# Stick-breaking attention in pairs of steps: turns and scores in 64-row tiles

## The chip, the cores and the metric

The kernel runs on one core of one Trainium2 chip. The metric is the device time of one execution in microseconds. The engines are named as the profile names them: PE (TensorE; PEld is its loading of weights), DVE (VectorE), ACT (ScalarE), POOL (GpSimd) and SP (SyncE, which here only issues DMAs).

## What is computed

One layer with a stick-breaking attention mixer over 2048 tokens of width 1024, with 16 heads of 64, and a final RMSNorm. All is float32.

```python
def stick_breaking_attention(q, k, v):
    """q,k,v: (B,S,H,Dh). A[t,s] = beta[t,s] * prod_{s<j<t} (1-beta[t,j]), s<t only."""
    ...
        z = jnp.einsum('bthd,bshd->bhts', q[:, t0:kend], k[:, :kend]).astype(jnp.float32) * scale
        mask = s_idx < t_idx
        log_beta = jax.nn.log_sigmoid(z)
        log_rem = jnp.where(mask, jax.nn.log_sigmoid(-z), 0.0)
        after = lax.cumsum(log_rem, axis=3, reverse=True) - log_rem
        w = jnp.where(mask, jnp.exp(log_beta + after), 0.0)
        outs.append(jnp.einsum('bhts,bshd->bthd', w.astype(v.dtype), v[:, :kend]))

def mixer_stick_breaking(h, w_in, w_out):
    proj = jnp.einsum('bsd,de->bse', h, w_in)
    q, k, v, g = jnp.split(proj, 4, axis=-1)
    o = stick_breaking_attention(q.reshape(hs), k.reshape(hs), v.reshape(hs)).reshape(B, S, SB_WIDTH)
    return jnp.einsum('bse,ed->bsd', o * jax.nn.silu(g), w_out)
```

The result is `rmsnorm(x + mixer(rmsnorm(x)))`.

## The kernel before

Every matrix product keeps float32 precision by splitting each operand into an upper part of reduced precision (`..._hi`) and the remainder (`..._lo`) and adding products of parts. The tokens are reversed on the host, so that the sum over later positions becomes a scan forward.

The program has four stretches. Up to about 184 us PE makes the values of all heads (line 713). Then it makes keys, queries and gates, in 96 groups of 24 products of 512 columns (`project`, line 764). From about 211 us the attention runs, with the rest of the projection spread between its steps (`filled(n)`: 3.344 products per step). From about 1466 us the gated output is multiplied with the output weights (`put_out`, line 851) and normalized.

The attention is a list of 640 steps (`STEPS`): for each of 16 heads, for query chunks c of 512 tokens, for key chunks j from c on, for four blocks r of 128 queries. Ten (c, j) units of four steps make a head; in the four units with j = c ("on the diagonal") the score widths of the four steps are 512, 384, 256 and 128 columns, and the widths of their turned pieces too; elsewhere all are 512. A step m passes through six operations:

- `scores` (PE, lines 782 and 784): two 128-row products into one of two banks `z_ps`. `k_parts` holds a head's keys in 64 rows of upper and 64 rows of lower parts, `q_parts` the queries in the same way, and `q_swapped` with the parts exchanged; so the two products sum all four products of parts.
- `stick` (ACT, L1003): the sigmoid, from `z_ps` into `u`.
- `scan` (DVE, L1236): the running product along the keys, in place.
- `turn` (PE, L794): transposes, 128 x 128 each, one for each of the four query blocks of the unit (fewer on the diagonal), into one of three banks `turn_ps`. It needs the scans of all blocks of the unit.
- `hi` (ACT, L1009) and `lo` (DVE, L1241): the upper and the lower part of the turned piece, out of the same bank.
- `weigh` (PE, L810 and L812): two products with the differences of the values (`dv_head`) into `o_ps`, which collects a chunk; `empty` (ACT, L1015) takes it out into one of two tiles `o_stage`.

The order is written by hand. Each engine has a loop over n, in which it does step n + 9 of the scores and sigmoids (`LEAD_SCORES`), n + 6 of the scans (`LEAD_SCAN`), n + 2 of the turns and upper parts (`LEAD_TURN`), and step n of the lower parts and the weighing, with the projection between. On PE a step is: scores, turn, project, weigh; where a score or weighing product has only 128 columns, a turn is put between the two. On DVE it is `made_low` (the lower part of a projection group, L1222 or L1220), scan, `lo`, then other parts such as `weight_lo` (L1212). SP loads keys (lines 528 and 529) and queries (539 and 540) a unit or more ahead; a load waits until the steps that used the place have their scores. At the beginning of the attention, at line 859, eight small transposes of 16 rows turn the first values; they are the only instructions on PE that don't use all 128 rows.

## Time and profile before

| | us |
|---|---|
| median of 3 runs | 1651.32 |
| lowest, highest | 1651.22, 1652.89 |
| the profiled execution | 1651.07 |
| its span, first to last instruction | 1649.3 |
| PE busy | 1638.1 (99%) |
| DVE busy | 1348.6 (82%) |
| ACT busy | 904.7 (55%) |

A row of PE has a start and a length, and the length contains the way of the last column through the array, so products in a row overlap in the records: what a product costs is the distance of its start to the next one's. The same holds on DVE and ACT to a lesser degree. "Idle before" is the time in which an engine had nothing running, and what released it.

### The profile page before, as it was taken

To read this page: it belongs to the slowest core of one execution; us is meant where nothing else is said; L and a number is where in the kernel's file an instruction comes from. 1 tells how busy PE (TensorE), PEld (TensorE's weight loads), DVE (VectorE), ACT (ScalarE), POOL (GpSimd) and SP (SyncE) were. 2 spreads that over 40 slices of the span, in tenths; PEclk is the share of its full clock that TensorE was granted. 3 is DMA by queue.
4 is the path that set the end of the run, shared out by engine and by line. 5 is a ranking of instruction groups with operands and counts; after the bars stand their busy time and mean duration, and the time that the engine had idled before them with its cause. 6 is when DMAs were issued, how large, how long until landed. Compare 5 with 4: busy or idle time off the path is not lost.

```text
span 1649.3 us, 23497 instructions
## 1 busy us (share of the span) xinstructions
PE 1638.1 (99%) x8642; PEld 1376.1 (83%) x8642; DVE 1348.6 (82%) x1901; ACT 904.7 (55%) x1782; POOL 165.5 (10%) x200
## 2 busy tenths in 40 slices
PE   9999999999999999999999999999999999999998
PEld 7888878888888888888888888888888888888887
DVE  5536369989898999899998999898889899957874
ACT  6625245655665566656565655656566656743221
POOL 0020020110111011101110211012011101000000
PEclk9999999999999999999999999999999999999999
DMA  9858643343424252434333333425242424779722
GB/s 314 276 163 277 190 142 108 110 126 92 150 68 136 69 154 80 132 94 124 109 98 106 120 113 90 132 87 147 58 147 81 144 77 129 247 259 363 247 105 87
DMA packets 164370, 237.10 MB, mean 144 GB/s; under 512 B 49952, under 2 KB 91936, under 8 KB 164256
## 3 DMA queue, kind: packets, MB, share of 16 engines
q1 hardware_dynamic: 94912, 160.29, 31.5%
q10 hardware_dynamic: 69344, 75.32, 14.6%
q8 instruction: 68, 1.11, 0.3%
q14 instruction: 46, 0.38, 0.1%
HBM read 155.78 MB, written 79.76 MB: 143 GB/s over the span
## 4 chain that ended last, share of the span: by engine, by line
PE 96%; DMA 2%; ACT 1%; DVE 0%; POOL 0%; issue 0%; SPq 0%; DVEq 0%
PE proj_ps L764 31%; PE turn_ps L794 15%; PE o_ps L810 8%; PE o_ps L812 8%; PE z_ps L784 8%; PE z_ps L782 8%; PE proj_ps L713 5%; PE turn_ps L851 3%; PE o_ps L713 3%; PE turn_ps L713 3%; PE z_ps L851 3%; PE proj_ps L851 2%; PE o_ps L851 1%; DMA gate<-gate_cols 1%; POOL w_raw L697 0%; DMA w_raw<-in_w_qkg 0%
## 5 line engine op out<-in xcount | busy, mean ns | idle before, releaser
L1003 ACT ACTIVATE u<-z_ps 128x512 f32<-128x512 f32 (+3 forms) x640 | 341.6, 534 | 365.4 <-PE z_ps L784 362.3
L1236 DVE TENSOR_TENSOR_SCAN u<-u,u 128x512 f32<-128x512 f32 x384 | 492.1, 1281 | 0.0
L1241 DVE TENSOR_TENSOR r_turned_lo<-turn_ps,r_turned_hi 128x512 fp32r<-128x512 f32 (+3 forms) x640 | 380.9, 595 | 103.5 <-ACT r_turned_hi L1009 99.5
L1009 ACT ACTIVATE r_turned_hi<-turn_ps 128x512 fp32r<-128x512 f32 (+3 forms) x640 | 341.0, 533 | 96.7 <-PE turn_ps L794 45.2
L794 PE MATMUL turn_ps<-ident,u 128*128 128x128 f32 x2176 | 352.6, 273 | 0.0
L764 PE MATMUL proj_ps<-hT_hi,w_hi 128*128 128x512 f32 x768 | 317.9, 414 | 0.0
L764 PE MATMUL proj_ps<-hT_hi,w_lo 128*128 128x512 f32 x768 | 317.7, 414 | 0.0
L764 PE MATMUL proj_ps<-hT_lo,w_hi 128*128 128x512 f32 x768 | 317.5, 413 | 0.0
L794 PEld LDWEIGHTS turn_ps<-ident,u 128*128 128x128 f32 x2176 | 266.8, 140 | 54.5
L697 POOL TENSOR_SCALAR w_raw<-w_raw,a_norm_col 128x128 f32<-128x128 f32 x192 | 163.7, 871 | 1201.3 <-DMA w_raw<-in_w_qkg 1201.3
L784 PE MATMUL z_ps<-k_parts,q_swapped 128*128 128x512 f32 (+3 forms) x640 | 235.8, 368 | 0.0
L782 PE MATMUL z_ps<-k_parts,q_parts 128*128 128x512 f32 (+3 forms) x640 | 235.7, 368 | 0.1
L812 PE MATMUL o_ps<-r_turned_lo,dv_head 128*128 128x512 f32 (+3 forms) x640 | 234.3, 366 | 0.0
L810 PE MATMUL o_ps<-r_turned_hi,dv_head 128*128 128x512 f32 (+3 forms) x640 | 230.5, 360 | 1.2 <-DVE r_turned_lo L1241 0.5
L1236 DVE TENSOR_TENSOR_SCAN u<-u,unbroken 128x512 f32<-128x512 f32 (+3 forms) x256 | 211.6, 827 | 0.0
L764 PEld LDWEIGHTS proj_ps<-hT_hi,w_lo 128*128 128x128 f32 x768 | 145.3, 189 | 17.8
L764 PEld LDWEIGHTS proj_ps<-hT_hi,w_hi 128*128 128x128 f32 x768 | 145.3, 189 | 17.3
L764 PEld LDWEIGHTS proj_ps<-hT_lo,w_hi 128*128 128x128 f32 x768 | 145.3, 189 | 17.2
L810 PEld LDWEIGHTS o_ps<-r_turned_hi,dv_head 128*128 128x128 f32 x640 | 120.1, 188 | 32.1 <-issue 2.2
L812 PEld LDWEIGHTS o_ps<-r_turned_lo,dv_head 128*128 128x128 f32 x640 | 120.5, 188 | 25.3
L782 PEld LDWEIGHTS z_ps<-k_parts,q_parts 128*128 128x128 f32 x640 | 120.2, 188 | 20.7 <-issue 0.7
L784 PEld LDWEIGHTS z_ps<-k_parts,q_swapped 128*128 128x128 f32 x640 | 120.8, 189 | 16.5
(138 smaller groups left out, 1601.1 us busy)
## 6 DMA issues: line engine op xcount, KB each, us to landing
qk_hi_cols<-made_hi ACTq DMA_DIRECT2D x64, 256.0 KB, 2.8
qk_lo_cols<-made_lo ACTq DMA_DIRECT2D x64, 256.0 KB, 2.7
x_T<-in_xT SPq DMA_DIRECT2D x29, 512.0 KB, 6.0
w_raw<-in_w_qkg SPq DMA_DIRECT2D x24, 512.0 KB, 3.7
x_rows<-in_x SPq DMA_DIRECT2D x16, 512.0 KB, 4.9
v_rows<-v_stage ACTq DMA_DIRECT2D x32, 256.0 KB
v_here<-v_rows SPq DMA_DIRECT2D x64, 128.0 KB, 3.1
v_next<-v_rows SPq DMA_DIRECT2D x64, 128.0 KB, 3.5
```

The source lines that it names most:

```text
L697: last = nc.gpsimd.tensor_scalar(w_raw[t % 2][:, k, :], w_raw[t % 2][:, k, :], norm_col[:, k:k + 1], None, ALU.mult)
L713: last = nc.tensor.matmul(v_ps[v % len(v_ps)][:], a[:, c, k, tok], b[:, k, :], start=(k == 0 and n == 0), stop=(k == KT - 1 and n == 2))
L764: last = nc.tensor.matmul(p_ps[g % RP][:], a[t % 2][:, k, :], b[:, c, k, :], start=(n == 0), stop=(n == QPM - 1))
L782: nc.tensor.matmul(out, q_parts[c % 2][:, tau], k_parts[:, sig], start=True, stop=False)
L784: nc.tensor.matmul(out, q_swapped[c % 2][:, tau], k_parts[:, sig], start=False, stop=True).then_inc(s_z, 1)
L794: last = nc.tensor.transpose(t_ps[m % RT][:, t * P:(t + 1) * P], u_t[unit][t][:, r * P - lo:(r + 1) * P - lo], ident[:])
L810: nc.tensor.matmul(o_ps[:, 0:w], weights, rt_hi[m % RT][:, 0:w], start=begin, stop=False)
L812: last = nc.tensor.matmul(o_ps[:, 0:w], weights, rt_lo[m % RT][:, 0:w], start=False, stop=end)
L1003: nc.scalar.activation(u_t[(m // CB) % RU][STEPS[m][3]][:, 0:w], z_ps[m % RZ][:, 0:w], ACT.Sigmoid, scale=-Z_SCALE).then_inc(s_u, 1)
L1009: nc.scalar.activation(rt_hi[m % RT][:, 0:w], t_ps[m % RT][:, 0:w], ACT.Copy).then_inc(s_hi, 1)
L1236: nc.vector.tensor_tensor_scan(u, u, other, start, ALU.mult, op).then_inc(s_r, 1)
L1241: nc.vector.tensor_tensor(rt_lo[m % RT][:, 0:w], t_ps[m % RT][:, 0:w], as_f32(rt_hi[m % RT][:, 0:w]), ALU.subtract).then_inc(s_lo, 1)
```

## The change

The attention goes in pairs of steps (`PAIR = 2`): every loop goes by two, PE's, ACT's and DVE's.

- Scores: the keys of a head lie in SBUF as upper parts twice (rows 0 to 63 and again 64 to 127, `k_hi_twice`) and lower parts twice (`k_lo_twice`). The queries of even blocks lie in rows 0 to 63, those of odd blocks in rows 64 to 127 (`q_hi`, `q_lo`). A product has 64 rows; the two steps of a pair alternate, in three rounds: upper x upper, lower x upper, upper x lower. The product of the two lower parts is left out.
- Turns: each 128 x 128 transpose becomes two, one from rows 0 to 63 and one from rows 64 to 127, of 64 columns each. The halves go to two banks of `turn_ps`, which hold both steps of a pair; the third bank (`spare_ps`) serves other stages. The first turn of the next pair waits for both lower parts of this one (`s_lo`).
- Order: PE does turns of a pair, scores of a pair, `weigh` of the first step, the projection of two steps, `weigh` of the second. ACT does two `hi`, two `stick`, then the rest; DVE two scans, two `lo`, then the rest. `hi` waits for the turns of both steps, the second one also until PE has weighed the first step of the pair before (`s_w`), whose tile `r_turned_hi` it overwrites. `lo` waits for both `hi`. No turn stands between narrow products any more.
- Leads: scores 10 steps ahead, scans 8, turns and both parts 2. `o_stage` has one tile, not two.
- Loads: four key loads per unit of keys, not two; four query loads of half the size, in rows of 128 tokens.

```diff
-LEAD_SCORES = 9
+PAIR = 2
+LEAD_SCORES = 10
 LEAD_TURN = 2
-LEAD_SCAN = 6
-RU, RZ, RT, RO, RP = 3, 2, 3, 2, 2
+LEAD_SCAN = 8
+RU, RZ, RT, RO, RP = 3, 2, 3, 1, 2
+HALF = P // 2
...
-        t_ps = [pb(f"turn_ps{n}") for n in range(RT)]
+        turn_ps = ctx.enter_context(nc.psum_tensor("turn_ps", [P, 2, CH], F32))
+        t_ps = [turn_ps[:, 0, :], turn_ps[:, 1, :], pb("spare_ps")]
...
-                    sp.dma_start(as_f32(k_parts[0:DH, cols]), qk_hi[rows, cols]).then_inc(s_k[j], 16)
-                    sp.dma_start(as_f32(k_parts[DH:P, cols]), qk_lo[rows, cols]).then_inc(s_k[j], 16)
+                    for tile, src in ((k_hi, qk_hi), (k_lo, qk_lo)):
+                        sp.dma_start(as_f32(tile[0:HALF, cols]), src[rows, cols]).then_inc(s_k[j], 16)
+                        sp.dma_start(as_f32(tile[HALF:P, cols]), src[rows, cols]).then_inc(s_k[j], 16)
...
+                def scores(m):
...
+                    if m >= RZ:
+                        pe.wait_ge(s_u, m - RZ + PAIR)
+                    tau = slice(r // PAIR * P, (r // PAIR + 1) * P)
+                    for n, (a, b) in enumerate(((q_hi, k_hi), (q_lo, k_hi), (q_hi, k_lo))):
+                        for odd in range(PAIR):
+                            rows = slice(odd * HALF, (odd + 1) * HALF)
+                            lo = score_cols(m + odd)
+                            sig = slice(j * CH + lo, (j + 1) * CH)
+                            last = nc.tensor.matmul(z_ps[(m + odd) % RZ][:, 0:CH - lo], a[c % 2][rows, tau], b[rows, sig],
+                                                    start=(n == 0), stop=(n == 2))
...
+                def turn(m):
...
+                    pe.wait_ge(s_r, m - m % CB + CB)
+                    if m and m % PAIR == 0:
+                        pe.wait_ge(s_lo, m)
+                    for t in range(turn_width(m) // P):
                         lo = t * P if j == c else 0
-                        last = nc.tensor.transpose(t_ps[m % RT][:, t * P:(t + 1) * P],
-                                                   u_t[unit][t][:, r * P - lo:(r + 1) * P - lo], ident[:])
+                        for half in range(2):
+                            rows = slice(half * HALF, (half + 1) * HALF)
+                            at = m % PAIR * PAIR * P + t * HALF
+                            last = nc.tensor.transpose(turn_ps[:, half, at:at + HALF],
+                                                       u_t[unit][t][rows, r * P - lo:(r + 1) * P - lo], ident[rows, rows])
...
+                for n in range(-LEAD_SCORES, NS, PAIR):
+                    if inside(n + LEAD_TURN):
...
+                        turn(n + LEAD_TURN)
+                        turn(n + LEAD_TURN + 1)
                     if inside(n + LEAD_SCORES):
+                        scores(n + LEAD_SCORES)
                     if inside(n):
+                        weigh(n)
+                    project(filled(n - 1), filled(n + 1))
+                    put_out(out_filled(n - 1), out_filled(n + 1))
+                    if inside(n):
+                        weigh(n + 1)
...
                 def hi(m):
-                    act.wait_ge(s_t, m + 1)
+                    act.wait_ge(s_t, m - m % PAIR + PAIR)
+                    if m % PAIR and m >= RT:
+                        act.wait_ge(s_w, (m - RT) // PAIR + 1)
...
                 def lo(m):
-                    dve.wait_ge(s_hi, m + 1)
+                    dve.wait_ge(s_hi, m - m % PAIR + PAIR)
```

How this moves instructions. PE before, in the attention, one step (the weighing of one step, scores of another, here 256 wide, four turns, three projection products, the next weighing):

```order
L810 MATMUL o_ps<-r_turned_hi_102,dv_head 128x512 [waits r_lo_ready]
L812 MATMUL o_ps<-r_turned_lo_105,dv_head 128x512
L782 MATMUL z_ps<-k_parts,q_parts_85 128x256 [waits u_ready]
L784 MATMUL z_ps<-k_parts,q_swapped_87 128x256
L794 MATMUL turn_ps<-ident,u_0_90 128x128 [waits scan_ready]
L794 MATMUL turn_ps<-ident,u_1_91 128x128
L794 MATMUL turn_ps<-ident,u_2_92 128x128
L794 MATMUL turn_ps<-ident,u_3_93 128x128
L764 MATMUL proj_ps<-hT_hi,w_hi_76 128x512
L764 MATMUL proj_ps<-hT_lo,w_hi_76 128x512
L764 MATMUL proj_ps<-hT_hi,w_lo_78 128x512
L810 MATMUL o_ps<-r_turned_hi_103,dv_head 128x512 [waits r_lo_ready]
```

PE after, in the attention: the last turns of the first step of a pair, those of the second (three blocks, on the diagonal), the scores of another pair off the diagonal, the first weighing:

```order
L819 MATMUL turn_ps<-ident,u_2_101 128x64 x2
L819 MATMUL turn_ps<-ident,u_3_102 128x64 x2
L819 MATMUL turn_ps<-ident,u_0_99 128x64 [waits scan_ready]
L819 MATMUL turn_ps<-ident,u_0_99 128x64
L819 MATMUL turn_ps<-ident,u_1_100 128x64 x2
L819 MATMUL turn_ps<-ident,u_2_101 128x64 x2
L801 MATMUL z_ps<-k_hi_twice,q_hi_87 128x512 [waits u_ready]
L801 MATMUL z_ps<-k_hi_twice,q_hi_87 128x512
L801 MATMUL z_ps<-k_hi_twice,q_lo_89 128x512 x2
L801 MATMUL z_ps<-k_lo_twice,q_hi_87 128x512 x2
L833 MATMUL o_ps<-r_turned_hi_103,dv_head 128x512 [waits r_lo_ready]
L834 MATMUL o_ps<-r_turned_lo_106,dv_head 128x512
```

What was scores, turn, projection, weighing in every step is now turns and scores of two steps in one block of 64-row instructions, and the 128-row instructions behind it. Before its first row here stands the first turn, which waits for `r_lo_ready`.

ACT before, over three steps, near the same place:

```order
L1003 ACTIVATE u_0_90<-z_ps 128x512 [waits scores_ready]
L1009 ACTIVATE r_turned_hi_104<-turn_ps 128x512 [waits turned]
L981 DMA qk_hi_cols<-made_hi 128x512 [waits made_hi_ready]
L1003 ACTIVATE u_1_91<-z_ps 128x512 [waits scores_ready]
L1009 ACTIVATE r_turned_hi_102<-turn_ps 128x512 [waits turned]
L1003 ACTIVATE u_2_92<-z_ps 128x512 [waits scores_ready]
L1009 ACTIVATE r_turned_hi_103<-turn_ps 128x512 [waits turned]
```

ACT after, over a pair and the beginning of the next:

```order
L978 ACTIVATE made_hi<-proj_ps 128x512 [waits made_high_stored,made_lo_ready,projected]
L1019 ACTIVATE r_turned_hi_104<-turn_ps 128x2x4x64 [waits turned]
L1019 ACTIVATE r_turned_hi_105<-turn_ps 128x2x4x64 [waits first_of_pair_weighed,turned]
L1012 ACTIVATE u_0_91<-z_ps 128x512 [waits scores_ready]
L1012 ACTIVATE u_1_92<-z_ps 128x512 [waits scores_ready]
L990 DMA qk_hi_cols<-made_hi 128x512 [waits made_hi_ready]
L961 ACTIVATE dv_head<-v_here_66 128x4x64 [waits o_ready,dv_ready]
```

Sigmoids and upper parts alternated; now both upper parts come first, the second with a wait of its own (`first_of_pair_weighed`), and the sigmoids stand behind it.

## Rows read from the trace of the kernel before

**Rows 1.** The page, part 1 (busy us, share, instructions) and part 4 (chain)

```profile
PE 1638.1 (99%) x8642; PEld 1376.1 (83%) x8642; DVE 1348.6 (82%) x1901; ACT 904.7 (55%) x1782; POOL 165.5 (10%) x200
...
PE 96%; DMA 2%; ACT 1%; DVE 0%; POOL 0%; issue 0%; SPq 0%; DVEq 0%
```

**Rows 2.** PE's waits, 300 to 1400 us: line <- releaser: total us, times, longest

```profile
PE o_ps L810 <- issue: 0.2, 1, 0.2
```

**Rows 3.** Windows: stretch, us, busy us (xcount) by engine, PEclk, DMA share, GB/s

```profile
700.00:1466.00 766.00, 765.28 (x4238) 646.65 (x4237) 692.93 (x939) 469.56 (x955) 82.59 (x96) 1.00 0.39 119
```

**Rows 4.** Timeline of PE: start, length (us), line, out<-in, shape, xcount

```profile
702.51 0.27 PE L794 MATMUL turn_ps<-ident,u 128*128 128x128 f32 x1
702.53 0.31 PE L812 MATMUL o_ps<-r_turned_lo,dv_head 128*128 128x128 f32 x1
...
705.33 0.39 PE L782 MATMUL z_ps<-k_parts,q_parts 128*128 128x512 f32 x1
705.56 0.40 PE L784 MATMUL z_ps<-k_parts,q_swapped 128*128 128x512 f32 x1
705.79 0.60 PE L794 MATMUL turn_ps<-ident,u 128*128 128x128 f32 x4
706.15 0.47 PE L764 MATMUL proj_ps<-hT_hi,w_hi 128*128 128x512 f32 x1
706.46 0.39 PE L764 MATMUL proj_ps<-hT_lo,w_hi 128*128 128x512 f32 x1
...
707.39 0.39 PE L782 MATMUL z_ps<-k_parts,q_parts 128*128 128x512 f32 x1
```

**Rows 5.** Timeline, PE and its weight loads (PEld), projection

```profile
704.40 0.39 PE L764 MATMUL proj_ps<-hT_lo,w_hi 128*128 128x512 f32 x1
704.40 0.19 PEld L764 LDWEIGHTS proj_ps<-hT_hi,w_lo 128*128 128x128 f32 x1
```

**Rows 6.** Timeline of PE, then of its loads, around the eight 16-row turns

```profile
210.95 0.39 PE L764 MATMUL proj_ps<-hT_hi,w_lo 128*128 128x512 f32 x1
211.27 0.67 PE L859 MATMUL turn_ps<-ident,v_first_rows 16*128 16x16 f32 x8
211.87 0.50 PE L782 MATMUL z_ps<-k_parts,q_parts 128*128 128x512 f32 x1
212.21 0.39 PE L784 MATMUL z_ps<-k_parts,q_swapped 128*128 128x512 f32 x1
...
211.27 0.57 PEld L859 LDWEIGHTS turn_ps<-ident,v_first_rows 16*128 16x128 f32 x8 [0.35 <-issue]
```

**Rows 7.** Groups by form: xcount | busy us, mean ns | idle before, releasers

```profile
L794 PE MATMUL turn_ps<-ident,u 128*128 128x128 f32 x2176 | 352.6, 273 | 0.0
...
L1241 DVE TENSOR_TENSOR r_turned_lo<-turn_ps,r_turned_hi 128x512 fp32r<-128x512 f32 x448 | 302.2, 674 | 66.8 <-ACT r_turned_hi L1009 63.6
...
L1009 ACT ACTIVATE r_turned_hi<-turn_ps 128x512 fp32r<-128x512 f32 x448 | 267.4, 597 | 40.4 <-PE turn_ps L794 33.5
...
L812 PE MATMUL o_ps<-r_turned_lo,dv_head 128*128 128x512 f32 x448 | 175.1, 391 | 0.0
...
L1222 DVE TENSOR_TENSOR made_lo<-proj_ps,made_hi 128x512 fp32r<-128x512 f32 x64 | 43.6, 682 | 19.4 <-ACT made_hi L969 15.8 <-DMA qk_lo_cols<-made_lo 3.4
...
L1212 DVE TENSOR_TENSOR w_lo<-w_raw,w_hi 128x1024 fp32r<-128x1024 f32 x24 | 29.4, 1224 | 8.7 <-ACT w_hi L958 8.5
```

**Rows 8.** Timeline of DVE: scans and lower parts without idle time between them

```profile
707.90 1.28 DVE L1236 TENSOR_TENSOR_SCAN u<-u,u 128x512 f32<-128x512 f32 x1
709.09 0.67 DVE L1241 TENSOR_TENSOR r_turned_lo<-turn_ps,r_turned_hi 128x512 fp32r<-128x512 f32 x1
709.67 1.28 DVE L1236 TENSOR_TENSOR_SCAN u<-u,u 128x512 f32<-128x512 f32 x1
```

**Rows 9.** Timeline: a lower part that waited for its upper part

```profile
718.64 0.59 ACT L1009 ACTIVATE r_turned_hi<-turn_ps 128x512 fp32r<-128x512 f32 x1
...
719.26 0.69 DVE L1241 TENSOR_TENSOR r_turned_lo<-turn_ps,r_turned_hi 128x512 fp32r<-128x512 f32 x1 [0.48 <-ACT r_turned_hi L1009]
```

More of the change, by code:

```diff
@@ L38 @@
 AT_Y = BASE + 16 * KB
-AT_X = BASE + 24 * KB
+AT_Q = [BASE + 82 * KB, BASE + 92 * KB]
 AT_U = BASE + 32 * KB
@@ L458, in v_stored, with turned, by_halves @@
             eng.wait_ge(s_vout[v % 2], sum(32 if n % NB else 16 for n in range(v % 2, v + 1, 2)))
+        def turned(m):
+            blocks = turn_width(m) // P
+            at = m % PAIR * PAIR * P
+            return turn_ps[:, :, at:at + blocks * HALF].rearrange("p half (t n) -> p half t n", n=HALF)
+        def by_halves(tile, m):
+            return tile[:, 0:turn_width(m)].rearrange("p (t half n) -> p half t n", half=2, n=HALF)
         def dv_free(eng, h, j):
@@ L537, in load_q @@
                     rows, cols = slice(h * DH, (h + 1) * DH), slice(c * CH, (c + 1) * CH)
-                    for tile, top, bottom in ((q_parts, qk_hi, qk_lo), (q_swapped, qk_lo, qk_hi)):
-                        sp.dma_start(as_f32(tile[c % 2][0:DH, :]), top[rows, cols]).then_inc(s_q[c % 2], 16)
-                        sp.dma_start(as_f32(tile[c % 2][DH:P, :]), bottom[rows, cols]).then_inc(s_q[c % 2], 16)
+                    for tile, src in ((q_hi, qk_hi), (q_lo, qk_lo)):
+                        blocks = src[rows, cols].rearrange("p (i two t) -> p two i t", two=PAIR, t=P)
+                        for odd in range(PAIR):
+                            here = as_f32(tile[c % 2][odd * HALF:(odd + 1) * HALF, :]).rearrange("p (i t) -> p i t", t=P)
+                            sp.dma_start(here, blocks[:, odd]).then_inc(s_q[c % 2], 16)
                 def chunk_stored(c):
@@ L796, in turn @@
-                    if blocks.stop == turn_width(m) // P:
-                        last.then_inc(s_t, 1)
-                def weigh(m, first):
+                        for half in range(2):
[3 more added lines that the diff above has]
+                                                       u_t[unit][t][rows, r * P - lo:(r + 1) * P - lo], ident[rows, rows])
@@ L800, in weigh @@
+                    last.then_inc(s_t, 1)
+                def weigh(m):
                     h, c, j, r = STEPS[m]
                     w = turn_width(m)
+                    if c == 0 and r == 0:
+                        pe.wait_ge(s_dlo, NC * h + j + 1)
                     begin, end = j == c and r == 0, j == NC - 1 and r == CB - 1
+                    if begin and NC * h + c:
+                        pe.wait_ge(s_ost, NC * h + c)
+                    pe.wait_ge(s_lo, m + 1)
                     weights = dv_head[:, j * CB + sigma_block(m), :]
[L804 to L811 removed]
+                    nc.tensor.matmul(o_ps[:, 0:w], weights, rt_hi[m % RT][:, 0:w], start=begin, stop=False)
@@ L812, in weigh @@
                     last = nc.tensor.matmul(o_ps[:, 0:w], weights, rt_lo[m % RT][:, 0:w], start=False, stop=end)
-                    if end:
+                    if m % PAIR == 0:
+                        last.then_inc(s_w, 1)
+                    elif end:
                         last.then_inc(s_o, 1)
@@ new lines, in _ @@
+                    for m in range(n, n + PAIR):
+                        for g in GROUPS_DONE.get(m, []):
+                            made_high(g)
+                        if m in HI_W:
+                            weight_hi(HI_W[m])
+                        if m in PAIR_HI:
+                            dv_hi(*PAIR_HI[m])
+                        if m in SUM_AT:
+                            piece_start(SUM_AT[m])
+                        if m in GATE_AT:
+                            piece_high(GATE_AT[m])
+                        if m in WO_HIGH_AT:
+                            out_weight_high(WO_HIGH_AT[m])
```

164 lines of the change are left out of this document (57 added, 107 removed).

## The prediction, made before the change was run

> **What bounds the kernel now.** I read the page's busy shares and its chain first. TensorE (PE) is busy 99% of the span and holds 96% of the chain [rows 1]; its waits from 300 to 1400 us add up to 0.2 us [rows 2]. The stretches show the same in the attention stage, with the granted clock at 1.00, thus at the 2.4 GHz level, and VectorE (DVE) next at 693 of 766 us [rows 3]. So the time is the sum of what PE issues, and any saving on PE counts until DVE, or a hand-over between engines, ends later. PE's own order in time gives the prices [rows 4]: starts of 512-column products lie 0.23 us apart (0.232 in this stage; a recorded length of 0.39 contains the drain and is no price). From the first of four turns (705.79) to the product after the next (706.46) are 0.67 us; less one product 0.44 are left, 0.109 us for each turn of 128 columns. A step is 705.33 to 707.39, 2.06 us with three projection products.
>
> The profiled execution took 1651.07 us (span 1649.3 and 1.8 around it), the median of the runs is 1651.32: I add changes to 1651.1.
>
> **Scores.** Two 128-row products per step become three rounds per pair of steps, in each of which both steps have one 64-row product. No row shows two tiles in one array at once. One bound is a round for the price of one product, the other is two products in series. I take the first, because the two have disjoint partitions for weights and columns and write two banks, so nothing of one is read or written by the other. Then the 192 pairs off the diagonal go from 4 x 0.232 to 3 x 0.232, -44.5 us; the 64 pairs of 512 and 384 columns from 0.82 to 0.70, -7.7; those of 256 and 128 gain nothing. Sum **-52 us**. In series each round would cost a second product: 192 x 3 x 0.232 = 134, 64 x 3 x 0.176 = 34, 64 x 3 x 0.06 = 12, together 180 us more than the first bound.
>
> The Trainium skill, "TensorE: Matmul & The Clock Gate", Part 3, reports 3.07 times the rate for four row tiles side by side. That stands on the side of the first bound; no run here shows it.
>
> **Turns.** 2176 transposes of 128 x 128 become 4352 of 64 x 128 with 64 moving columns. A pass over 64 columns is half of 0.109, 0.055 us. The weight load has a row too: eight 16-row turns with 16 columns [rows 6] have their loads in 0.57 us, of which the last is 0.14, so 0.061 apart, where the pass is too short to matter. If the loads of two tiles go side by side as their passes do, a block costs 0.061 (the longer of load and pass), a saving of 2176 x 0.048 = **-104 us**. If they go one after the other, a block costs 2 x 0.061 = 0.122, +28 us. I take the first: the only new resource is the row group, and the issue of instructions is not the limit, since in a narrow step a product starts 0.02 us after a turn, with its load between them [rows 4]. The other end stays in the range.
>
> **Leaving and entering the 64-row form.** The same rows price this, and it is the term that the change's text doesn't show. From 210.95 to 212.21 PE does one projection product, eight small turns and one score product: 1.26 - 2 x 0.23 - 8 x 0.061 = 0.31 us over [rows 6]. Elsewhere a load starts with the product before it [rows 5]; here the first small load starts 0.32 after that product, and behind them the first score product takes 0.34 in place of 0.23: loads don't run ahead across the change of form. The new order has turns and scores together, and weighing and projection behind them, so one round trip per pair: 320 x 0.31 = **+99 us**. Bounds: nothing (it might be a matter of 16 rows, not of 64), and 0.40 if the drain of a full 512-column product counts on both sides.
>
> PE's work so changes by -52 - 104 + 99 = **-57 us**.
>
> **The hand-over.** Before, three turn banks let PE run ahead. Now a pair's turns share two banks, and the next pair's turns wait for both lower parts of this pair (the wait on r_lo_ready at the first turn). Also ScalarE's (ACT) second upper part waits until PE has weighed the first step of the pair before, which is queued behind this pair's scores. The chain from turn to turn, off the diagonal: entry 0.12, turns 8 x 0.061 = 0.49, scores 0.70, exit 0.19, weighing 0.23 to its second product, 0.39 to that one's end, the second upper part 0.60, the two lower parts 0.58 [rows 8] and 0.67 [rows 7], and 0.03 at each of three hand-overs [rows 9]: 4.06 us. PE's own work per pair there is 0.31 + 0.49 + 0.70 + 4 x 0.232 + 6.69 x 0.232 = 3.98 (2 x 3.344 projection products per pair by the filling rate); before it was 4.28. So PE waits 0.08 in such a pair. On the diagonal PE's work is short while the pair turned is already a wide one: worked out for the 20 pairs of a head, the chain is longer by 0.08 in six, 0.09 in three, 0.44 in three and 0.20 in one. That is 2.3 us per head, **+36 us** for 16.
>
> **VectorE.** Per pair it has two scans, 1.19 apart to the lower part behind, and two lower parts, 0.58: 3.56 us [rows 8], under 4.06. Its other work comes in lumps: 22 weight parts of 1.2 us [rows 7] (1.14 apart from the next) make such a pair 4.70, 0.64 x 22 = 14 us; the 91 lower parts of projections (0.68, 0.59 apart) alone make it 4.15, and with a second lump 4.5, about 11 us in all. Before, PE's three turn banks took these up, now they can't: **+25 us**.
>
> At no cost: the key loads double and the query loads stay as many with half the bytes, in a stage whose DMA share is 0.39 [rows 3]; they are asked for many steps ahead, and what is queued behind them on SP is asked for as early. Were that cover gone, a late key chunk would stop PE for some us once a head. Output stores with one staging tile have a chunk of steps, over 6 us, to land. Strided reading of two banks by ACT and DVE has the same 512 elements.
>
> **Sum**: 1651.1 - 57 + 36 + 25 = 1655 us. Gain and price nearly cancel; the sign hangs on two prices that have no row of their own form.
>
> **Rivals.**
> 1. *The change of form is cheap* (64-row tiles need no more than half of 0.31, or their loads run ahead). For it: the row is of 16-row turns behind a load that also waited for data. Against it: both its edges show the lost run-ahead. At 0.15 PE's work falls by 48 more, of which about 33 arrive (the chain has entry and exit in it too, the pairs that DVE bounds have not): 1622 us; at nothing, twice that, 1590.
> 2. *The weight loads of the two tiles go in series* (slower). Place: the turns. A block costs 0.122, and since turns lie on PE's path and on the chain alike, it passes through but for the pairs that DVE bounds: 2176 x 0.061 = 133, about 113 after those: 1768 us. It decides the sign from 0.061 on: each 0.01 us on a block is 20 us, and 0.052 would already make the kernel faster by 1%.
> 3. *The tiles don't run side by side at all*: then three products in place of two, and the turns in series. 1768 + 180 = 1948; with the scores alone in series 1655 + about 165 = 1820.
> 4. *A weight load can't hide behind its own tile's product.* Its length is the 0.11 by which the first score product in [rows 6] is late. Three rounds x 320 x 0.11 = 106, and the turns back at 0.061 + 0.055 per block, + 100: 1860 us. Against it, over the full array a load starts with the product before it on the same rows [rows 5].
>
> The Trainium skill, "TensorE: Matmul & The Clock Gate", Part 3 (The mechanism), has rival 4 as a rule: loads overlap running matmuls only where the row group differs. By that rule products over all rows could not hide their loads; the trace disagrees for the full array, and no row tells it for tiles, so the rival keeps a small chance.
>
> **How the numbers follow.** Forecast as summed, with its own range 1635 to 1685 (0.01 us on a block is 20 us; the hand-over could be taken up in part; ACT's parts of weights, which I count at nothing behind its idle time, could add): 0.45. Rival 1: 0.20. Rival 2 (with blocks between 0.08 and 0.122): 0.22. Rivals 3 and 4: 0.08. Something unseen: 0.05, both ways. What a measurement of this kernel can tell from no change is about 0.2%, 3.3 us: 1648 to 1654.6. Of the forecast's 0.45 I put 0.15 under, 0.09 within and 0.21 over that; rival 1 is faster. With the rest, faster 0.37, same 0.11, slower 0.52. Left out of the range 1605 to 1772 are the cheapest change of form, and rivals 3 and 4, under 0.2.
>
> **What would show it.** Side by side scores: starts of the two products of a round within some hundredths, rounds 0.23 apart. Turns: eight blocks in 0.5 us (right) or 1.0 (rival 2). Change of form: the first load of a turn about 0.09 after the stream before it ends, and the first weighing product behind the scores taking 0.34. Hand-over: idle time of PE ahead of the first turn of a pair, released by DVE's lower part, some 0.1 to 0.4 at a time; in it ACT's second upper part waiting for the weighing. The forecast is wrong if PE still has no waits, or if its busy sum without waits moves by more than 30 us from -57.

## The result, and the profile after

The changed kernel takes **1759.2 us** in the median of four runs (1757.31 to 1759.96), the kernel before beside it 1651.63 (1651.22 to 1652.89): a ratio of 1.0651, 95% interval 1.0638 to 1.0664. The sum forecast 1655. The sign with the larger chance came, and the time lies inside the range, but 104 us above the forecast, next to rival 2's 1768. The range reached that far only because of rival 2, so the question is whether rival 2 happened or the sum was wrong elsewhere.

The page, parts 1 and 4, against [rows 1]:

```profile
PE 1635.7 (93%) x11458; PEld 1243.3 (71%) x11458; DVE 1346.6 (77%) x1901; ACT 888.5 (51%) x1782; POOL 150.9 (9%) x200
...
PE 65%; DVE 16%; ACT 7%; issue 5%; ACTq 3%; DMA 2%; POOL 1%; SPq 0%; DVEq 0%
```

TensorE held 96% of the chain before and now 65%. No other engine has become the bound: VectorE's share of busy time fell too. The same stretch as in [rows 3], from the windows (us, busy us and count by engine, PEclk, DMA share, GB/s), shows all engines less busy, and the granted clock no longer at 1.00:

```profile
700.00:1466.00 766.00, 711.14 (x5568) 525.71 (x5566) 644.02 (x874) 419.79 (x874) 82.39 (x104) 0.99 0.35 102
```

The waits of the whole span (engine, what waited, its releaser: us in total, times, longest). PE's row, the last, takes the place of the 0.2 us in [rows 2]; 75 of its 102.9 us fall in the same stretch, 300 to 1400 us. ACT and DVE waited before the change too, but PE did not wait for them.

```profile
ACT r_turned_hi L1019 <- PE turn_ps L819: 285.1, 245, 6.9
DVE r_turned_lo L1253 <- ACT r_turned_hi L1019: 211.1, 218, 3.6
ACT r_turned_hi L1019 <- PE o_ps L834: 193.4, 256, 2.2
PE turn_ps L819 <- DVE r_turned_lo L1253: 102.9, 156, 6.2
```

Each of ACT, DVE and PE waits for the one before it in the circle turn, upper part, lower part. Such a circle has one pair in flight, and where it is longer than each engine's own work its length sets the time. 102.9 us is a lower bound for PE's part: a wait that lies under the recorded drain of the product before it doesn't show. Worked out from starts, over all 320 pairs (from the start of the product before to the first turn, less that product's columns at the full clock and the 0.12 that an entry without a wait takes), PE waits about 130 us (128 to 131, by the price taken for the columns): 49 in the 192 pairs whose turns follow a weighing of 512 columns (median 0.16 each), and some 80 in the 128 that follow one of 384 or 128 columns, where a diagonal unit is weighed (medians 0.3 and 0.5).

PE's timeline of one pair off the diagonal (start, length, line, out<-in, shape, count), against [rows 4]:

```profile
701.39 0.40 PE L834 MATMUL o_ps<-r_turned_lo,dv_head 128*128 128x512 f32 x1
701.86 0.71 PE L819 MATMUL turn_ps<-ident,u 64*128 64x64 f32 x16
702.35 0.50 PE L801 MATMUL z_ps<-k_hi_twice,q_hi 64*128 64x512 f32 x2
702.67 0.42 PE L801 MATMUL z_ps<-k_hi_twice,q_lo 64*128 64x512 f32 x2
702.90 0.42 PE L801 MATMUL z_ps<-k_lo_twice,q_hi 64*128 64x512 f32 x2
703.25 0.50 PE L833 MATMUL o_ps<-r_turned_hi,dv_head 128*128 128x512 f32 x1
703.59 0.40 PE L834 MATMUL o_ps<-r_turned_lo,dv_head 128*128 128x512 f32 x1
...
706.16 0.65 PE L819 MATMUL turn_ps<-ident,u 64*128 64x64 f32 x14 [0.30 <-DVE r_turned_lo L1253]
```

Sixteen half turns take 0.49 us (701.86 to 702.35), 0.061 for a block of two: the side-by-side price, not rival 2's 0.122. The two products of a round start within 0.04 of each other and so make one row ("x2"), and rounds are 0.23 apart (702.67, 702.90): rival 3 is out. The first round is the exception with 0.32. Behind the scores the exit (from the 64-row form back to 128 rows) shows twice, 0.35 and 0.34 for products that elsewhere take 0.23. The weight loads of the same stretch say why:

```profile
701.83 0.60 PEld L819 LDWEIGHTS turn_ps<-ident,u 64*128 64x128 f32 x16 [0.48 <-issue]
702.43 0.22 PEld L801 LDWEIGHTS z_ps<-k_hi_twice,q_lo 64*128 64x128 f32 x2
702.67 0.21 PEld L801 LDWEIGHTS z_ps<-k_lo_twice,q_hi 64*128 64x128 f32 x2
703.25 0.19 PEld L833 LDWEIGHTS o_ps<-r_turned_hi,dv_head 128*128 128x128 f32 x1 [0.36 <-issue]
703.36 0.19 PEld L834 LDWEIGHTS o_ps<-r_turned_lo,dv_head 128*128 128x128 f32 x1
```

A load of the 64-row form starts while the product of the same rows runs (702.43 under 702.35, 702.67 with the product), so rival 4 is out too. But no load crosses the change of form: the one of 703.25 starts only with its own product, and the next one 0.11 later, where in [rows 5] it starts with the product before. The Trainium skill, "TensorEngine Tiling (Array Packing)", Key Properties, says that changing the tiling mode drains TensorE. The trace agrees in that no load runs ahead across the change (703.25). What the change costs is read below.

The other half of the circle, ACT and DVE at the same time:

```profile
704.09 0.60 ACT L1019 ACTIVATE r_turned_hi<-turn_ps 128x512 fp32r<-128x512 f32 x1 [0.89 <-PE o_ps L834]
...
704.72 1.29 DVE L1253 TENSOR_TENSOR r_turned_lo<-turn_ps,r_turned_hi 128x512 fp32r<-128x512 f32 x2 [0.64 <-ACT r_turned_hi L1019]
```

The second upper part waits for the weighing's second product of 703.59, the lower parts for it, the next turns (706.16) for them.

### The profile page after: what moved, and what is told of

It reads as the page before. It is cut to its first block, busy times and chain, and to the rows that moved or that the text cites. A ratio compares the mean times of both kernels' runs of the same rounds, so it can differ in the third digit from the quotient of the medians.

```text
span 1758.2 us, 29895 instructions
## 1 busy us (share of the span) xinstructions
PE 1635.7 (93%) x11458; PEld 1243.3 (71%) x11458; DVE 1346.6 (77%) x1901; ACT 888.5 (51%) x1782; POOL 150.9 (9%) x200
## 4 chain that ended last, share of the span: by engine, by line
PE 65%; DVE 16%; ACT 7%; issue 5%; ACTq 3%; DMA 2%; POOL 1%; SPq 0%; DVEq 0%
PE proj_ps L781 15%; PE z_ps L801 9%; PE turn_ps L819 9%; DVE r_turned_lo L1253 9%; PE o_ps L833 7%; PE proj_ps L730 5%; PE o_ps L834 5%; DVE u L1249 5%; ACT r_turned_hi L1019 4%; PE proj_ps L869 3%; PE o_ps L730 2%; PE spare_ps L730 2%; PE z_ps L869 2%; PE turn_ps L869 2%; ACTq L1032 2%
## 5 line engine op out<-in xcount | busy, mean ns | idle before, releaser
L1253 DVE TENSOR_TENSOR r_turned_lo<-turn_ps,r_turned_hi 128x512 fp32r<-128x512 f32 (+3 forms) x640 | 359.3, 603 | 212.3 <-ACT r_turned_hi L1019 211.1
L1249 DVE TENSOR_TENSOR_SCAN u<-u,u 128x512 f32<-128x512 f32 x384 | 472.7, 1272 | 0.0
L819 PEld LDWEIGHTS turn_ps<-ident,u 64*128 64x128 f32 x4352 | 169.2, 139 | 213.7 <-issue 207.5
L819 PE MATMUL turn_ps<-ident,u 64*128 64x64 f32 x4352 | 205.6, 229 | 113.0 <-DVE r_turned_lo L1253 102.9
L1012 ACT ACTIVATE u<-z_ps 128x512 f32<-128x512 f32 (+3 forms) x640 | 306.2, 538 | 1.0 <-PE z_ps L801 1.0
L833 PE MATMUL o_ps<-r_turned_hi,dv_head 128*128 128x512 f32 (+3 forms) x640 | 265.0, 414 | 0.0
L801 PE MATMUL z_ps<-k_hi_twice,q_hi 64*128 64x512 f32 (+3 forms) x640 | 150.7, 443 | 1.1 <-ACT u L1012 1.1
L801 PE MATMUL z_ps<-k_lo_twice,q_hi 64*128 64x512 f32 (+3 forms) x640 | 132.1, 366 | 0.0
L801 PE MATMUL z_ps<-k_hi_twice,q_lo 64*128 64x512 f32 (+3 forms) x640 | 127.6, 364 | 0.0
L1183 DVE TENSOR_TENSOR hT_lo<-x_T,hT_hi 128x1024 fp32r<-128x1024 f32 x29 | 35.5, 1224 | 53.8 <-ACT hT_hi L925 53.4
```

Source lines behind the costliest of these rows:

```text
L801: last = nc.tensor.matmul(z_ps[(m + odd) % RZ][:, 0:CH - lo], a[c % 2][rows, tau], b[rows, sig], start=(n == 0), stop=(n == 2))
L819: last = nc.tensor.transpose(turn_ps[:, half, at:at + HALF], u_t[unit][t][rows, r * P - lo:(r + 1) * P - lo], ident[rows, rows])
L833: nc.tensor.matmul(o_ps[:, 0:w], weights, rt_hi[m % RT][:, 0:w], start=begin, stop=False)
L1012: nc.scalar.activation(u_t[(m // CB) % RU][STEPS[m][3]][:, 0:w], z_ps[m % RZ][:, 0:w], ACT.Sigmoid, scale=-Z_SCALE).then_inc(s_u, 1)
L1249: nc.vector.tensor_tensor_scan(u, u, other, start, ALU.mult, op).then_inc(s_r, 1)
L1253: nc.vector.tensor_tensor(by_halves(rt_lo[m % RT][:], m), turned(m), by_halves(as_f32(rt_hi[m % RT][:]), m), ALU.subtract).then_inc(s_lo, 1)
```

## The experiments

All are compared with the kernel before on the same chip (medians 1650.7 to 1651.4). Times are medians of four runs.

**Weighing before the turns.** The circle has scores and one weighing between a turn and the second upper part. This version weighs the pair's first step ahead of the turns, except where a chunk begins.

```
                 for n in range(-LEAD_SCORES, NS, PAIR):
+                    if inside(n) and not begins(n):
+                        weigh(n)
...
                     if inside(n + LEAD_SCORES):
                         scores(n + LEAD_SCORES)
-                    if inside(n):
+                    if begins(n):
                         weigh(n)
```

> The changed kernel (1759 us) with one call moved: PE weighs the first step of a pair before the turns of the next pair, not behind their scores, except in the 64 pairs that begin a chunk. ACT's second upper part then finds its wait long fulfilled. Theory A (the hand-over chain through that wait makes 1759): the chain off the diagonal falls from 4.30 to about 3.3 us, under PE's own 3.9, so the pair takes 3.9 and the time falls to 1625 to 1665 us. Theory B (what costs is DVE and ACT work in lumps, with a chain that is short anyway): no more than 30 us fall, 1730 or above.

Measured: 1697.82 (1694.85 to 1699.33), ratio 1.028 (1.0265 to 1.0295): 61 us of the 108 come back by an order of instructions alone. That lies between the two theories: the hand-over is the largest single part, but not all. Its PE timeline, with no wait at all in this pair, gives the price of the form:

```profile
651.99 0.39 PE L834 MATMUL o_ps<-r_turned_lo,dv_head 128*128 128x512 f32 x1
652.31 0.71 PE L819 MATMUL turn_ps<-ident,u 64*128 64x64 f32 x16
652.83 0.48 PE L801 MATMUL z_ps<-k_hi_twice,q_hi 64*128 64x512 f32 x2
653.15 0.40 PE L801 MATMUL z_ps<-k_hi_twice,q_lo 64*128 64x512 f32 x2
653.38 0.39 PE L801 MATMUL z_ps<-k_lo_twice,q_hi 64*128 64x512 f32 x2
653.70 0.50 PE L781 MATMUL proj_ps<-hT_hi,w_hi 128*128 128x512 f32 x1
654.04 0.39 PE L781 MATMUL proj_ps<-hT_lo,w_hi 128*128 128x512 f32 x1
...
656.43 0.34 PE L819 MATMUL turn_ps<-ident,u 64*128 64x64 f32 x4
```

Each start-to-start time over 0.232 is price: into the turns 0.32, so 0.09; first round 0.32, 0.09; out of the scores 0.32, 0.09; next product 0.34, 0.11. That is **0.38 us** per pair, one trip into the form and out again, where the prediction had 0.31. The pair from 652.31 to 656.43 is 4.12 us with seven projection products; the sum's prices give 4.05. Its waits:

```profile
PE o_ps L833 <- DVE r_turned_lo L1258: 33.0, 31, 5.6
PE turn_ps L819 <- DVE r_turned_lo L1258: 14.0, 20, 2.2
```

The wait for lower parts has partly moved from the turns to the weighing that now stands ahead of them.

**Less work on PE, in the changed kernel.** If PE were the bound, removed work would come back whole; if the circle is, only what stands in it. The first leaves the third round of scores out (it is in the circle), the second one in eight of the projection products (outside it; `n % 7 == 3` holds for 3 of the 24 products of a group).

```
-                    for n, (a, b) in enumerate(((q_hi, k_hi), (q_lo, k_hi), (q_hi, k_lo))):
+                    for n, (a, b) in enumerate(((q_hi, k_hi), (q_lo, k_hi))):
```

> The changed kernel with the third round of scores (upper x lower) left out, so the scores lack that product. Theory A: a round lies on the chain ahead of the weighing, so nearly all of it comes off: 192 x 0.23 + 64 x 0.18 + 64 x 0.12 = 63 us at most, 50 to 63 expected, thus about 1700. Theory B: pairs that DVE bounds give nothing back, 20 to 40 us. If the two tiles of a round ran one after the other, it would be 100 us or more.

Measured: 1719.34, ratio 1.042 (1.0397 to 1.0444), 40 of at most 63 us less than the changed kernel. That is the upper end of theory B and 10 us short of theory A's range. The granted clock was lower here (0.987 against 0.993, medians of four runs), which cost at most 10 us; what kept the rest isn't shown.

```
                     for i in range(start, stop):
                         g, n = i // QPM, i % QPM
                         t, c = GROUPS[g]
+                        if i >= BEFORE * QPM and n % 7 == 3:
+                            continue
```

> The changed kernel with one in seven of the projection products between the steps left out (312 products, so keys, queries and gates lack terms). They stand behind the first weighing on PE. Theory A: PE waits there anyway, so of 312 x 0.232 = 72 us only some 5 to 25 come back, 1735 to 1755. If PE's own work bounded the pairs, all 72 would: 1687.

Measured: 1745.32, ratio 1.0568 (1.0552 to 1.0583). The expectation counted 312 products; the trace has 11458 - 11185 = 273 fewer, which at 0.232 are 63 us of PE's work, and 14 came back. So of two equal pieces of PE's work, the one in the circle gave 40 us back and the one beside it 14: in most pairs the circle bounds, not PE.

**Whole turns.** Only the turns go back to 128 rows and columns; scores stay in tiles.

```
-                        for half in range(2):
-                            rows = slice(half * HALF, (half + 1) * HALF)
...
+                        last = nc.tensor.transpose(turn_ps[:, m % PAIR, t * P:(t + 1) * P],
+                                                   u_t[unit][t][:, r * P - lo:(r + 1) * P - lo], ident[:])
```

> The changed kernel with its turns made whole again (128 x 128, one bank for each step of a pair), everything else as changed; the change of form then lies between turns and scores, as many times. If the halves of a turn run side by side, a block goes from about 0.065 back to 0.109 us on the chain: 2176 x 0.044 = 96, thus 70 to 110 us slower, 1830 to 1870. If turning in halves gains nothing, 1759.

Measured: 1870.12, ratio 1.1322 (1.1305 to 1.1339), 111 us slower than with half turns. The prediction gave the half turns 104 us of gain; this confirms it and ends rival 2. PE's timeline:

```profile
700.68 1.06 PE L814 MATMUL turn_ps<-ident,u 128*128 128x128 f32 x8 [0.34 <-DVE r_turned_lo L1248]
701.67 0.49 PE L799 MATMUL z_ps<-k_hi_twice,q_hi 64*128 64x512 f32 x2
```

Eight whole turns and the entry take 0.99; 0.87 for the turns leaves 0.12, the 64-row entry in its new place.

**One more change of form.** The weighing-first version, with one projection product of each pair between the turns and the scores (none added, one moved).

```
+                    between = min(filled(n - 1) + 1, filled(n + 1))
+                    project(filled(n - 1), between)
                     if inside(n + LEAD_SCORES):
                         scores(n + LEAD_SCORES)
```

> The first experiment's kernel (weighing first, 1698 us) with one projection product of every pair moved between its turns and its scores: the same instructions, but one more leaving and entering of the 64-row form per pair. Theory: the change of form costs a round trip of 0.3 to 0.38 us on PE, which bounds most pairs there, so 320 x 0.3 to 0.38 less what waits take up: 1775 to 1820 us. If a change of form costs nothing and it is only the first load that can't run ahead, under 1740.

Measured: 1772.39, ratio 1.0736 (1.072 to 1.0752), 74.6 us over the weighing-first version, 0.233 for each of 320 pairs, just under what was expected. In its order of PE:

```profile
700.80 0.71 PE L819 MATMUL turn_ps<-ident,u 64*128 64x64 f32 x16
701.44 0.49 PE L781 MATMUL proj_ps<-hT_lo,w_hi 128*128 128x512 f32 x1
701.87 0.50 PE L801 MATMUL z_ps<-k_hi_twice,q_hi 64*128 64x512 f32 x2
```

From the first turn to the first score 1.07 us, against 0.52 in the version without (652.31 to 652.83). Less the product's 0.232, the trip costs 0.32. Listed waits on lower parts fell from 47 to 28 us; with those 19, 94 us of 102 (320 x 0.32) are accounted for. So a trip into the 64-row form and out costs about a third of a microsecond, whatever waits there are beside it.

**Shorter scans.** Half the columns of each scan left out, which takes 285 us off VectorE's busy time (1346.6 to 1062.1; the expectations said 250 and 190): once in the changed kernel, once with the weighing first.

```
-                    u = u_t[(m // CB) % RU][r][:, 0:CH - score_cols(m)]
+                    u = u_t[(m // CB) % RU][r][:, 0:(CH - score_cols(m)) // 2]
```

> The changed kernel (1759 us) with each scan over the first half of its columns alone (the weights of the other half are then raw sigmoids): DVE has about 250 us less to do. If the hand-over chain bounds the pairs, DVE isn't in it with its scans, and only the pairs with lumps gain: 10 to 30 us off, 1730 to 1750. If DVE's work bounds them, 80 us or more.

Measured: 1732.46, ratio 1.0493 (1.0475 to 1.051), 27 us less.

> The kernel with the weighing first (1698 us) with half scans. What DVE's work costs there comes off: of some 60 us of PE's waits and 46 us over the kernel before. If DVE's lumps are what holds it, 1650 to 1670; if PE's own work (with a round trip of 0.38 in place of 0.31) and the granted clock are, it stays over 1675.

Measured: 1668.17, ratio 1.0106 (1.009 to 1.0121), 30 us less. VectorE is not the bound: 285 us less work gave a tenth of it. The 27 us of the changed kernel fit the 25 that the prediction had for VectorE's lumps of other work, but shorter scans help every pair in which VectorE ends late, so they are an upper bound for the lumps and not their measure.

**Weight parts on the idle engine.** The weighing-first version, with 22 of VectorE's 24 weight parts on GpSimd, which goes on scaling the raw weights in the same loop.

```
+                    if n in LO_W:
+                        t = LO_W[n]
+                        pool.wait_ge(s_whi, t + 1)
+                        nc.gpsimd.tensor_tensor(w_lo[t % 2][:], w_raw[t % 2][:], as_f32(w_hi[t % 2][:]), ALU.subtract).then_inc(s_wlo, 1)
```

> The kernel with the weighing first, with the lower parts of the 22 later weight tiles made by POOL, not by DVE: 22 lumps of 1.14 us leave DVE, and POOL is idle nine tenths. 10 to 25 us off 1698 if such lumps are waited for; nothing, or slower, if POOL takes so long that the weights come late.

Measured: 1705.53, ratio 1.0334 (1.0319 to 1.035), 8 us slower than without. The lumps are gone from VectorE, yet PE's listed waits on lower parts rose from 47 to 56 us. The timeline of VectorE and GpSimd shows why the move gained nothing:

```profile
886.02 4.54 DVE L1265 TENSOR_TENSOR_SCAN u<-u,u 128x512 f32<-128x512 f32 x2
886.24 3.24 POOL L724 TENSOR_TENSOR w_lo<-w_raw,w_hi 128x1024 fp32r<-128x1024 f32 x1 [4.80 <-ACT w_hi L983]
```

Two scans elsewhere take 2.45 us (718.70 in the same run). Of the scans off the diagonal (`u<-u,u`), the 23 that ran beside one of GpSimd's parts took 2.18 us each on average and the others 1.27. Over all its instructions that is some 33 us more, against the 27 us of the 22 parts it no longer makes, and VectorE's busy time rose from 1342.9 to 1349.7 us. That this is the whole of the 8 us isn't shown; a part on GpSimd also takes 2.7 us in place of 1.2.

**Scores first, then stores first.** Instead of moving a weighing, the scores go ahead of the turns and so out of the circle:

```
                 for n in range(-LEAD_SCORES, NS, PAIR):
+                    if inside(n + LEAD_SCORES):
+                        scores(n + LEAD_SCORES)
                     if inside(n + LEAD_TURN):
...
                         turn(n + LEAD_TURN + 1)
-                    if inside(n + LEAD_SCORES):
-                        scores(n + LEAD_SCORES)
```

> The changed kernel with scores ahead of the turns in each pair, nothing else. The chain from turn to turn then has no scores in it (0.8 us less, 3.5 off the diagonal), and the scores fill the time in which PE waited for the lower parts. The theory of the chain: as fast as or a little faster than weighing first (1698), 1680 to 1700, since the pairs that begin a chunk are helped too. If the gain of that kernel came from something else in its order, this one stays near 1759.

Measured: 1697.05, ratio 1.0278 (1.0263 to 1.0293), as expected: the same 62 us by another way. On top of that, ACT asks for its DMA stores of projections before the upper parts, not behind the sigmoids:

```
                     for m in range(n, n + PAIR):
+                        for g in GROUPS_DONE.get(m - PAIR, []):
+                            store_high(g)
+                        for g in MADE_LOW.get(m - PAIR, []):
+                            store_low(g)
+                    for m in range(n, n + PAIR):
                         if inside(m + LEAD_TURN):
                             hi(m + LEAD_TURN)
```

> The kernel with the scores first, and ACT's stores of projection parts put ahead of its two upper parts. DVE and ACT wait in some groups for the store of the group before; if those waits reach PE, 5 to 15 us off; if not, the same within 3 us.

Measured: 1678.98 (1677.06 to 1679.38), ratio 1.0166 (1.0149 to 1.0183), 18 us less, more than expected. In the version without this, VectorE waited 9.6 us in three places for a gate store to have landed before it could write the next lower part of a projection; that wait is gone from the list, and PE's on lower parts at the turns fell from 16.9 to 7.7 us. Of the 18 us, PE's listed waits account for 14, so the earlier store seems to shorten the circle through VectorE. No full kernel with the change was faster than this one by more than the noise. What PE still waits for:

```profile
PE z_ps L801 <- ACT u L1012: 36.0, 51, 2.6
PE turn_ps L819 <- DVE r_turned_lo L1253: 7.7, 12, 2.7
```

The circle's waits are nearly gone; now the scores wait for ACT. One of the 51, in PE's timeline and ACT's:

```profile
941.15 0.34 PE L834 MATMUL o_ps<-r_turned_lo,dv_head 128*128 128x384 f32 x1
942.37 0.50 PE L801 MATMUL z_ps<-k_hi_twice,q_hi 64*128 64x512 f32 x2 [0.87 <-ACT u L1012]
...
937.83 0.60 ACT L1025 ACTIVATE o_stage<-o_ps 128x512 f32<-128x512 f32 x1 [0.51 <-PE o_ps L834]
938.46 0.46 ACTq L1031 DMA_DIRECT2D o_hi_cols<-o_stage  x1
938.96 0.61 ACTq L1032 DMA_DIRECT2D o_lo_cols<-o_stage  x1
939.70 0.60 ACT L978 ACTIVATE made_hi<-proj_ps 128x512 fp32r<-128x512 f32 x1 [1.27 <-issue]
940.19 0.41 ACT L961 ACTIVATE dv_head<-v_here 128x256 fp32r<-128x256 f32 x1
...
940.69 0.55 ACT L1019 ACTIVATE r_turned_hi<-turn_ps 128x256 fp32r<-128x256 f32 x2
941.13 1.09 ACT L1012 ACTIVATE u<-z_ps 128x512 f32<-128x512 f32 x2
```

At the end of a chunk ACT copies the output, issues two stores (1.1 us of its queue's time), makes an upper part of a projection and of the values' differences and the two upper parts of the turned pieces, and only then reaches the sigmoids that free the score banks.

**Later pieces.** On top of that, the first four pieces of the output projection come four steps later.

```
-PIECE_STEP = [SHORT_FROM + 8, SHORT_FROM + 11, SHORT_FROM + 14, LAST_K_FROM + 4] + [REST_FROM + at for at in (6, 7, 8, 10)]
+PIECE_STEP = [SHORT_FROM + 12, SHORT_FROM + 15, SHORT_FROM + 18, LAST_K_FROM + 8] + [REST_FROM + at for at in (6, 7, 8, 10)]
```

> As the kernel with scores and stores first, and the first four pieces of the gated output made four steps later. In the traces so far DVE waits some 5 us for the load of the output parts in front of the first piece, and with one pair of turn banks PE stands behind it. 4 to 8 us off if that is so.

Measured: 1678.41, ratio 1.0168 (1.0153 to 1.0183): no difference, where 4 to 8 us were expected; where the first pieces stand is not what this version loses time on.

**Shorter scans in the fastest version.** The edit is the one shown for the scans.

> The stores-first version (1679 us, of which 28 us are left over the kernel before), with every scan over the first half of its columns: half of VectorE's scan work, about 190 us, is left out, so the output isn't the reference's; all of TensorE's and ScalarE's work stays. Theory A (what is left over is mostly VectorE ending last in the pairs that hold lumps of other work, so that shorter scans uncover them): 1645 to 1660 us, and TensorE's idle time ahead of the turns and scores nearly gone. Theory B (what is left over is TensorE's own: its work with the change of form, the lower clock after waits, the ends of the program): it stays over 1668 us. At 1650 or less TensorE's own work with the change would be no longer than before the change.

Measured: 1663.64 (1660.89 to 1664.58), ratio 1.0069 (1.0053 to 1.0086), 15 us less, between the two theories. The waits of its PE:

```profile
PE z_ps L801 <- ACT u L1012: 35.2, 54, 2.6
PE turn_ps L819 <- DVE r_turned_lo L1253: 2.6, 2, 2.0
```

The circle's waits have gone, ACT's have stayed. Its span is 1661.9; without these 37.8 us it would be 1624, 25 under the 1649.3 of before. That is a measure of what the change does to PE's own work, on the low side, since the list leaves out waits that lie under a recorded drain.

## Why the prediction was right or wrong, point by point

**Right: the scores.** Two tiles side by side, a round for the price of one product. Not foreseen was the 0.09 by which the first round is longer.

**Right: the turns.** 0.061 us a block as priced from the row of small turns in [rows 6]; 104 us forecast, 111 lost when they were undone. Rival 2 gave nearly the measured time, but its mechanism did not happen, and it was for its sake that the range reached to 1772: that the time lies inside is luck. A time that fits proves no mechanism.

**Too low: the change of form.** 0.38 us in place of 0.31 per pair: 320 x 0.07 = 22 us. The two exit prices and the entry were in [rows 6]; the first round behind small turns was not, since there the scores had another form. So PE's work fell by about 57 - 22 = 35 us by this pair, by 25 by the last experiment, and not by 57: of the 156 us that tiles save, the form takes 320 x 0.38 = 122. The prediction would have called itself wrong if this fall were more than 30 us off 57; it is 22 or 32 off, at the edge.

**The step that failed: the hand-over.** The prediction named the circle, its members and its order rightly, and summed it to 4.06 us, which is 0.08 over PE's own work. Measured, it is 4.30 (701.86 to 706.16). Term by term:

- first turn to the second weighing product: 1.61 forecast, 1.73 measured (703.59), of which 0.09 is the first round;
- from there to the upper part: 0.42 forecast, 0.50 measured (704.09);
- upper part to lower parts: 0.63 both;
- lower parts and entry: 1.40 forecast, 1.44 measured.

Each error is small, and all have one sign. Since PE's own work is almost as long, a circle 0.24 longer isn't 6% more waiting but several times as much: PE waited about 130 us, where 36 + 25 = 61 were forecast. This pair speaks for the 192 whose turns follow a weighing of 512 columns: 4.30 less the 4.05 of PE's own work there is 0.25, the mean of the 49 us found in them. The other 80 lie at the diagonals, where the prediction expected 36 at most, and there the circle was not taken apart term by term. The experiments carry the mechanism: taking one weighing or the scores out of the circle gave 61 or 62 us back, and 63 us of PE's work beside it gave 14. The 25 us for VectorE's lumps are not contradicted (27 from shorter scans, an upper bound).

**Not in the sum: ACT's queue.** The prediction counted ACT's other work at nothing behind its idle time. Asking for its stores earlier gave 18 us, and the output's copy and stores at each chunk end still cost up to 36 us in that version. ACT is half idle, but it stands in the circle, so what is queued ahead of an upper part is paid. Its parts of weights, which the prediction counted at nothing, are among it. The wait shown under the next point ended so late because ACT stood before such a part, whose input GpSimd had not finished, with two upper parts queued behind it:

```profile
736.72 1.06 ACT L967 ACTIVATE w_hi<-w_raw 128x1024 fp32r<-128x1024 f32 x1 [2.84 <-POOL w_raw L714]
```

Such waits of ACT are few (three, 7.9 us). PE's two longest waits (6.4 and 5.8 us by starts, at 1498.96 and 1563.87) stand behind VectorE's two waits of 5 us for a gate store (1494.6 and 1560.5), the kind that the earlier stores removed.

**Not in the sum: the clock.** Before, the granted clock was 1.00 from 200 to 1500 us. In the changed kernel, PE waited 1.78 us for lower parts; the score rounds right behind are still 0.23 apart (739.82, 740.05), but the projection products that came 2 us later lie 0.42 apart, the 1.2 GHz level. From PE's timeline, and a window, within which the level rises again (0.66 on average):

```profile
736.89 0.34 PE L834 MATMUL o_ps<-r_turned_lo,dv_head 128*128 128x384 f32 x1
739.01 0.68 PE L819 MATMUL turn_ps<-ident,u 64*128 64x64 f32 x15 [1.78 <-DVE r_turned_lo L1253]
...
739.82 0.43 PE L801 MATMUL z_ps<-k_hi_twice,q_lo 64*128 64x512 f32 x2
740.05 0.60 PE L801 MATMUL z_ps<-k_lo_twice,q_hi 64*128 64x512 f32 x2
...
741.61 0.63 PE L781 MATMUL proj_ps<-hT_hi,w_hi 128*128 128x512 f32 x1
742.03 0.63 PE L781 MATMUL proj_ps<-hT_lo,w_hi 128*128 128x512 f32 x1
...
741.40:744.60 3.20, 3.16 (x26) 2.53 (x25) 3.20 (x6) 1.87 (x4) 0.00 (x0) 0.66 0.22 82
```

The mean clock is 0.991 after and 0.999 before: some 28 us more at the lower level, which cost at most 14. Over four runs each it is 0.991 to 0.993 in the changed kernel and with the weighing first alike, 0.994 to 0.995 with stores first and 0.997 to 0.998 with short scans there. So fewer waits mostly go with a higher clock, but the weighing first took most of the waits away and left the clock as it was.

**The sum again**, from measured terms: 1651 - 35 (PE's work) + 128 (waits ahead of turns) + about 10 (clock; an estimate, at most 14) = 1754, against 1759. The terms are from one execution each, and waits and clock were not separated by an experiment.

**What stays open.** Of the 28 us that the fastest version is slower than before, the scans show 15 to hang on VectorE and the trace puts up to 36 at waits for ACT's sigmoids, nearly all at chunk ends, against the gain of 25 on PE's work. A version that frees the score banks earlier at chunk ends, by one more bank or by output copies elsewhere, wasn't tried, so whether the change can win is not known. No version measured here beats the kernel before.

## What to carry to other kernels

When a tuned engine is 99% busy and a change cuts its work and its buffers at once, compare the longest circle of hand-overs with the engine's own work per round: within a few per cent of each other, each small error in the circle is paid in full, so leave slack or take work out of the circle by reordering before counting on the gain. Keep all small-tile work in one block per round, since each trip into the form and out cost about a third of a microsecond here. Price a form from the nearest row of the same size of load and pass, which for the turns was right to the hundredth and for the change of form 0.07 us short, and add something for what stands first behind each switch. And before work goes from VectorE to GpSimd, look at what VectorE's instructions take beside it: here more than was taken away.

## What the runs showed of the hardware that was not expected

- Two 64-row tiles load and pass together: sixteen loads and sixteen 64-column passes in 0.49 us, 0.031 for each. In tiles a load also runs under the product of its own rows (702.43 under 702.35). The Trainium skill, "TensorE: Matmul & The Clock Gate", Part 3 (The mechanism), says that loads overlap running matmuls only where the row group differs, though a sentence above that it also names loads into a background weight buffer. With that "only" the trace disagrees, for 64-row tiles as for the full array in [rows 5].
- A switch between 128-row and 64-row form costs 0.09 us in, 0.09 and 0.11 on the first two products out, and 0.09 on the first full product round after small turns (weighing first, 652.31 to 654.04).
- VectorE's instructions took longer beside one on GpSimd: scans of 512 columns 2.18 us beside a subtraction of 1024 columns, and 1.27 without it.
- The lower clock level came after waits, not with them: the wait ended at 739.01, PE worked at the 2.4 GHz level until 740.05 at least, and only then did starts move apart.
